# Quarter-array local products and a reordered preparation in the recurrence of an attention/RWKV-7 encoder

## The reference, cut to what matters

```python
decay = exp(-exp(-softplus(-(w0 + tanh(w_l) @ w2)) - 0.5))
a = sigmoid(a0 + a_l @ a2)
kk = heads(k * k_k);  kk = kk / max(sqrt(sum(kk * kk, -1)), 1e-12)
k = k * (1.0 + (a - 1.0) * k_a)
y = wkv7(r, decay, k, v, -kk, kk * a)
# wkv7, for each frame and head:
sa = einsum('hvk,hk->hv', state, at)
state = state * wt + sa (x) bt + vt (x) kt
y_t = einsum('hvk,hk->hv', state, rt)
y = group_norm(y) * ln_w + ln_b + sum(r * k * r_k, -1) * v
```

## Time and profile before

| | before |
|---|---|
| timed runs, median (lowest, highest) | 1804.3 us (1803.42, 1804.86) |
| the profiled execution's own time | 1807.21 us |
| its span, mean granted TensorE clock | 1805.4 us, 0.979 |
| TensorE busy | 1738.3 us, 96% |
| VectorE busy | 988.2 us, 55% |
| ScalarE busy | 796.3 us, 44% |
| GpSimd busy | 693.3 us, 38% |
| chain that ended last, by engine | PE 85%, DVE 7%, DMA 3%, ACT 3%, issue 2% |

### The profile page before, as it was taken

The page is one execution under the profiler, slowest core; times in us unless marked ns, Lnnn a source line. Parts: engine busy times, 40 slices in busy tenths (PEclk is TensorE's granted clock), DMA queues, the critical chain, the costliest instruction groups (busy, mean ns, idle before and its releaser), DMA issues.

```text
span 1805.4 us, 30026 instructions
## 1 busy us (share of the span) xinstructions
PE 1738.3 (96%) x11960; PEld 1321.0 (73%) x11960; DVE 988.2 (55%) x1551; ACT 796.3 (44%) x1519; POOL 693.3 (38%) x502
## 2 busy tenths in 40 slices
PE   7999999999998998999999999999999999999997
PEld 4766666665575766768888768878888888888886
DVE  6543232325464756453340462388856775884788
ACT  5313233235342443541120232467666666756763
POOL 2211202010120111223333103398686876968772
PEclk9999999998989999999999999999999999999999
DMA  5101000000212114051211102202202022030202
GB/s 206 47 24 33 22 35 13 21 5 18 54 20 43 26 40 110 27 205 38 79 47 49 33 0 65 75 25 70 77 29 83 24 70 66 28 93 25 70 1 93
DMA packets 81681, 94.36 MB, mean 52 GB/s; under 512 B 53648, under 2 KB 56208, under 8 KB 81552
## 3 DMA queue, kind: packets, MB, share of 16 engines
q1 hardware_dynamic: 81552, 92.56, 16.7%
HBM read 82.57 MB, written 9.98 MB: 51 GB/s over the span
## 4 chain that ended last, share of the span: by engine, by line
PE 85%; DVE 7%; DMA 3%; ACT 3%; issue 2%; POOL 1%; SPq 1%; DVEq 0%; ACTq 0%; POOLq 0%
PE PS L1652 33%; PE PS L934 16%; PE PS L994 8%; PE PS L1095 3%; PE PS L1113 2%; PE PS L1134 2%; PE PS L1599 2%; PE PS L1168 1%; PE PS L1577 1%; PE PS L1444 1%; PE PS L1459 1%; DMA xt_dram<-sc_s 1%; PE PS L1171 1%; PE PS L1359 1%; PE PS L1302 1%
## 5 line engine op out<-in xcount | busy, mean ns | idle before, releaser
L1652 PE MATMUL PS<-memr,wsp 128*128 128x512 f32 x1332 | 319.9, 391 | 2.4 <-POOL wsp L895 2.4
L934 PE MATMUL PS<-xn,wsp 128*128 128x512 f32 x1344 | 309.1, 391 | 6.7 <-DVE xn L2212 6.7
L934 PEld LDWEIGHTS PS<-xn,wsp 128*128 128x128 f32 x1344 | 252.8, 189 | 62.8 <-DVE xn L2212 5.9
L1652 PEld LDWEIGHTS PS<-memr,wsp 128*128 128x128 f32 x1332 | 249.7, 188 | 57.7 <-POOL wsp L895 3.3
L776 POOL CAST wsp<-wraw 128x1024 fp32r<-128x1024 f32 x40 | 42.7, 1068 | 468.8 <-PE PS L934 302.3
L1652 PE MATMUL PS<-memr,wraw_r 128*128 128x512 f32 x684 | 165.7, 391 | 0.7 <-POOL wraw_r L895 0.7
L994 PE MATMUL PS<-xn,wsp 128*128 128x512 f32 x576 | 149.5, 407 | 3.3 <-DVE proj L2261 3.1
L895 POOL TENSOR_TENSOR wsp<-sa,wsp 128x512 fp32r<-128x512 f32 x86 | 115.2, 1342 | 89.9 <-ACT wsp L2103 89.8
L1652 PEld LDWEIGHTS PS<-memr,wraw_r 128*128 128x128 f32 x684 | 128.2, 188 | 29.1 <-POOL wraw_r L895 1.1
L994 PEld LDWEIGHTS PS<-xn,wsp 128*128 128x128 f32 x576 | 106.4, 192 | 41.4 <-issue 20.7
L1776 ACT ACTIVATE H<-PS,mst 128x128 f32<-128x128 f32 (+3 forms) x64 | 47.5, 743 | 184.9 <-DVE mst L2342 179.7
(11 more groups left out here) (349 smaller groups left out, 3170.3 us busy)
## 6 DMA issues: line engine op xcount, KB each, us to landing
wraw<-in_weights_dram SPq DMA_DIRECT2D x40, 512.0 KB, 3.6
sa<-in_weights_dram SPq DMA_DIRECT2D x32, 512.0 KB, 4.2
H<-in_x_dram SPq DMA_DIRECT2D x16, 512.0 KB, 6.7
sbx<-in_weights_dram SPq DMA_DIRECT2D x32, 256.0 KB, 2.9
sa<-in_weights_dram SPq DMA_DIRECT2D x32, 256.0 KB, 2.8
H<-in_weights_dram SPq DMA_DIRECT2D x8, 512.0 KB, 6.5
out_dram<-sbx SPq DMA_DIRECT2D x16, 256.0 KB, 2.1
a_dram<-H SPq DMA_DIRECT2D x16, 128.0 KB, 2.5
```

The source lines that it names most:

```text
L934: last = nc.tensor.matmul(PS[:, 2 * k + half, :], wsp[:, k, kt, a, :], src[:, at, b, HALF * half:HALF * half + HALF], start=(i == 0 and (a ...
L1652: last = nc.tensor.matmul(PS[:, g % PS_BANKS, :], w[:, a, win(k)], x[:, b, :], start=(k == 0 and (a, b) == (0, 0)), stop=(k == ROWS - 1 an ...
```

## The change

It has five parts.

1. **Local products.** In `local` the selection product of the other chunk took all 128 rows of the array at once (`slice(0, P)`). Now each selection product has 64 rows; the second one of each head moves out of `local` into a new step `other_r` behind both windows' `local`, which waits for `local`'s products by TensorE's own count `lo`. `other_r(b)` stands between `carry(a)` and `carry(b)`. The number of matmuls is the same, 16 a window.
2. **Order and engines of the preparation.** Slots and engines before → after: kk DVE 3 → ACT 9; na DVE 4 → ACT 3; b DVE 16 → POOL 13; rt POOL 17 → 14; kksq 5 → 4 (straight from the projection); ks0, ks1 6, 7 → 5, 6; kf 10 → 7; W, Wi 10, 11 → 8; wt 12 → 10; afirst 17 → 13; t1p, L 3 → 4; am 4 → 5; nkk 14 → 12; k2 5 → 13; al0 to al3 18–21 → 17–20; rk 21 → 22; x0, x1 24 → 23; substitution ends in 30 in place of 33; bonus 31, 32 → 33, 34. `beside_heads` follows.
3. **Function tables of ScalarE.** One table with both Ln and Exp is named ahead of the Ln in the head, before attention and in slot 6 of the preparation. The program's `ACT_TABLE_LOAD` instructions fall from 29 to 14. The load for tanh in pairs 1 to 3 now stands behind ScalarE's wait for lw0.
4. **Start of the recurrence.** Slots 0 to 3 of `beside(0, ..)` stand ahead of the doubling, on TensorE and VectorE, in place of between its steps.
5. **SyncE** waits for `tok{p-1}_7` before it loads `o_places[p]`, from pair 1 on.

```diff
-SUBST = {26: (0, 1, 2, 3), 27: (4, 5, 6, 7), 29: (8,), 30: (9,), 31: (10, 11), 32: (12, 13), 33: (14,)}
-BONUS = 31
+SUBST = {26: (0, 1, 2, 3), 27: (4, 5, 6, 7), 28: (8, 9, 10, 11), 29: (12, 13), 30: (14,)}
+BONUS = 33
@@ beside_heads
-                return ((0,), (1,), (2,), (3, 4), (5, 6), (7, 8, 9), (10, 11), (12, 13, 14), (15, 16, 17))[i]
-            return ((), (18, 19), (20, 21, 22), (24,), (), (26, 27), (29, 30, 31), (32, 33), ())[i - 9]
+                return ((0,), (1,), (2,), (3, 4), (5, 6), (7, 8, 9), (10, 11), (12, 13), (14, 15, 16))[i]
+            return ((), (17, 18), (19, 20), (21, 22, 23), (), (26, 27), (28, 29, 30), (33, 34), ())[i - 9]
@@ TensorE, local
-                    for c, rows in ((h, chunk(h)), (1 - h, slice(0, P))):
-                        last = nc.tensor.matmul(to_r(c), con[rows, C_SEL + CH * h:C_SEL + CH * h + CH],
-                                                rAR[p % 2][rows, w, 1, chunk(c)], start=False, stop=True)
-                last.then_inc(L_PE.sem, L_PE.one(f"ry{p}_{w}"))
+                    for c in range(2):
+                        from_k(h, c)
+                    last = from_r(p, w, h, h)
+                last.then_inc(L_PE.sem, L_PE.one(f"lo{p}_{w}"))
+
+            def from_r(p, w, h, c):
+                rows = slice(HD * h, HD * h + HD)
+                return nc.tensor.matmul(PS[0:HD, 2 + 2 * (w % 2) + c, CH * h:CH * h + CH],
+                                        con[rows, C_SEL + CH * h:C_SEL + CH * h + CH],
+                                        rAR[p % 2][rows, w, 1, chunk(c)], start=False, stop=(h != c))
+
+            def other_r(p, w):
+                r_at(L_PE, f"lo{p}_{w}")
+                for h in range(2):
+                    last = from_r(p, w, h, 1 - h)
+                last.then_inc(L_PE.sem, L_PE.one(f"ry{p}_{w}"))
@@ TensorE, the recurrence
+            for s in range(4):
+                beside(0, s)
             for lv in range(LEVELS):
                 for w in range(2):
                     double_q(lv, 0, w)
-                beside(0, 2 * lv)
                 for w in range(2):
                     double_z(lv, 0, w)
-                beside(0, 2 * lv + 1)
...
-                    for k, stage in enumerate((solve, local, carry)):
-                        for w in ab:
-                            stage(p, w)
-                        beside(p, t + 4 + k)
+                    for w in ab:
+                        solve(p, w)
+                    beside(p, t + 4)
+                    for w in ab:
+                        local(p, w)
+                    other_r(p, ab[0])
+                    carry(p, ab[0])
+                    other_r(p, ab[1])
+                    beside(p, t + 5)
+                    carry(p, ab[1])
+                    beside(p, t + 6)
@@ ScalarE, prep
-                if s == 5:
-                    r_at(P_DVE, f"kk_{n}")
+                if s == 3:
+                    r_at(P_ACT, f"ta1_{n}")
+                    nc.scalar.activation(rA, rA, ACT.Copy, scale=-0.5, bias=-0.5).then_inc(sem_, one("na"))
+                if s == 4:
...
-                    nc.scalar.activation(rBh[i], rKK, ACT.Square).then_inc(sem_, one("kksq"))
+                    nc.scalar.activation(rBh[i], proj[:, T_K + n, :], ACT.Square, scale=vech[:, 8 + n:9 + n]).then_inc(
+                        sem_, one("kksq"))
+                if s == 6:
+                    nc.scalar.preload_act_table_set("natural_log_exp_and_others")
```

More of the change, by code:

```diff
@@ L477, in build @@
                                            "rk0", "rk1"]))
-        P_ACT = Steps(sem("prep_act"), each(["tw0", "tw1", "ta0", "ta1", "kksq", "kl0", "kl1", "W", "kf", "Wi", "wt0", "wt1", "afirst"]))
+        P_ACT = Steps(sem("prep_act"), each(["tw0", "tw1", "ta0", "ta1", "na", "kksq", "kl0", "kl1", "kf", "W", "Wi", "kk", "wt0", "wt1", "afirst"]))
         P_DVE = Steps(sem("prep_dve"), each(
[L480 to L483, removed]
+            ["t1p", "L", "am", "nkk", "k2", "at", "bt", "kt", "al0", "al1", "al2", "al3", "rk", "x0", "x1"]
+            + [y for place in SUBST for j in SUBST[place] for y in (f"xm{j}", f"xa{j}")] + ["xt", "bv0", "bv1"]))
+        P_POOL = Steps(sem("prep_pool"), each(["b", "rt", "kh", "bh"]))
         O_PE = Steps(sem("post_pe"), each(["vs0", "vs1", "lg0", "lg1"]))
@@ new lines, in to_r, with to_y, from_b, from_k @@
+                def to_r(h, c):
+                    return PS[0:HD, 2 + 2 * s + c, CH * h:CH * h + CH]
+                def to_y(h, c):
+                    return PS[HD:P, 2 + 2 * s + c, CH * h:CH * h + CH]
+                def from_b(h, c, to, cols):
+                    nc.tensor.matmul(to, rPG[s][chunk(c), h, cols], rSC[s][chunk(c), h, 0, :], start=(h == 0), stop=False)
+                def from_k(h, c):
+                    return nc.tensor.matmul(to_y(h, c), rVZ[s][chunk(c), h, HD:P], rSC[s][chunk(c), h, 2, :],
+                                            start=False, stop=(h == 1))
@@ L1713, in _ @@
             act.wait_ge(eps_made, 1)
-            nc.scalar.activation(small[:, 41:42], small[:, 40:41], ACT.Ln)
             for half in range(2):
@@ L1831, in prep @@
                     nc.scalar.activation(rB[i][:, halves(s - 6)], PS[:, 7, :], ACT.Ln).then_inc(sem_, one(f"kl{s - 6}"))
-                if s == 10:
+                if s == 7:
+                    r_at(P_ACT, f"kl1_{n}")
+                    nc.scalar.activation(rB[i], rB[i], ACT.Exp, scale=-0.5).then_inc(sem_, one("kf"))
+                if s == 8:
                     r_at(P_DVE, f"L_{n}")
@@ L1837, in prep @@
                     nc.scalar.activation(rW, rWi, ACT.Exp, scale=-half_e).then_inc(sem_, one("W"))
-                    r_at(P_ACT, f"kl1_{n}")
-                    nc.scalar.activation(rB[i], rB[i], ACT.Exp, scale=-0.5).then_inc(sem_, one("kf"))
-                if s == 11:
                     r_at(P_ACT, f"W_{n}")
                     nc.scalar.activation(rWi, rWi, ACT.Exp, scale=half_e).then_inc(sem_, one("Wi"))
-                if s == 12:
+                if s == 9:
+                    nc.scalar.activation(rKK, proj[:, T_K + n, :], ACT.Copy, scale=vech[:, 8 + n:9 + n]).then_inc(
+                        sem_, one("kk"))
+                if s == 10:
                     if n >= 2:
```

93 lines of the change are left out of this document (39 added, 54 removed).

## The result

The changed kernel takes 1814.06 us (median of 5 runs, 1811.47 to 1821.45), the kernel before in the same comparison 1803.42 (5 runs, 1794.47 to 1804.86): ratio 1.0085, 95% interval 1.006 to 1.011. It is slower, by 10.6 us between the medians and by some 15 us as the ratio has it; 1785.5 was forecast. The profiled execution took 1814.06 us, its span is 1812.3, the mean clock 0.968. That is 6.9 us more than the profiled execution of the kernel before, which at 1807.21 us was itself slower than all five timed runs: the two traces show a part of the loss.

A forecast was written before the change was run, and what follows sets the result against it. TensorE's own products were taken to set the recurrence's pace, busy 257 of 285 us. Gains and losses summed to −18.8 us from the 1804.3 us median, giving 1785.5 us, range 1775 to 1797.

The forecast's parts named there:

- Moves to GpSimd: Recurrence preparation: b on GpSimd starts 6.8 us before bt needs it, so 0; up to 1 us a pair if late.
- Head: Start of the kernel: one table load of 1.28 us between Ln and Exp goes and counts whole, −1.3 us.
- The tanh load: Pairs 1 and 2: table load behind the lw0 wait, 1.28 us each; with na on ScalarE, +4.7 us (0 to +7).
- The local products: Sixteen groups in the recurrence: quarter form −1.1 us each, −17.6; 4.95 returns as waits, net −12.6 us.
- Pair boundaries: Solved blocks load before TensorE asks: three waits go, −7.55, half clock behind them, −6.7; together −14.2 us, upper bound 0.
- End of attention: Head 7, block 7: rk1 waits for bv0, +4.0 us (0 to +5.3), and half clock behind it, +1.7 (0 to 3.4).
- The stall: TensorE at the end of head 7: idle about 3.1 us before rk1, until VectorE's bv0 has read bank 7.
- Start of the recurrence: End of attention to first solve: 20.6 us in place of 20.9, −0.3 us (−3 to +3).
- The slower rival: Recurrence: more, shorter waits lower the clock; slower from a mean clock of 0.88, 1810 us or more; chance 0.04.
- five new waits: TensorE in the recurrence: own-count wait, ks1, al0, tanh and na, named as what could lower the clock.

The follow-up runs named there:

- e2_bdve: The changed kernel with b back on VectorE and rt back in slot 17 on GpSimd: 1796.8 us, ratio 0.9978.
- e9_rtfirst: The changed kernel with rt issued ahead of b on GpSimd (slot 12), b still on GpSimd: 1802.6 us, ratio 1.0017.
- e3: The changed kernel with rk0 and bv0 of pair 0 moved to query block 6 of head 7, one substitution slot to block 5: 1815.1 us, ratio 1.0073.
- e4: The changed kernel with the first four slots of the recurrence back between the doubling's steps on TensorE and VectorE: 1810.8 us, ratio 1.0069.
- e8: The changed kernel with rt alone back in slot 17, b still on GpSimd: 1814.9 us, ratio 1.0077.
- e13: The changed kernel with tanh's table named ahead of ScalarE's wait for lw0, nothing else: 1805.65 us, ratio 1.0032.
- e10_tanh: e2_bdve with tanh's table named ahead of ScalarE's wait for lw0, na staying on ScalarE: 1785.2 us, ratio 0.9915.
- e14_tables: The kernel before with one table for Ln and Exp named in slot 6 of ScalarE's preparation, nothing else: 1810.4 us against 1799.3, ratio 1.0063.
- e6_all: e2_bdve with tanh's table named ahead of the wait, na back on VectorE, and the edits of e3 and e4: 1782.75 us, ratio 0.9883.
- e11_oldlocal: e6_all with the old local products: 1799.65 us against 1801.6 for the kernel before, ratio 0.9991.
- e1_local: The kernel before with the quarter-form local products, other_r and their order from the change, nothing else: 1792.5 us against 1799.9, ratio 0.9957.

## Why the prediction was wrong

- **Moves to GpSimd.** This step failed worst. "GpSimd works 53 of 285 us, and b (some 2 us) starts four slots, 6.8 us, before bt needs it: 0", with an upper bound of 1 us a pair. Idle time of GpSimd was read as room. Undoing it gives 17 us (e2_bdve), 11 of them by freeing rt alone (e9_rtfirst). I had looked at neither what runs on VectorE at that time, nor what b's new wait holds up behind it in GpSimd's stream; the 1.90 us of L2212 beside L778 stood in the trace of the kernel before. The half clock goes with it. In the five kernels with both operations beside VectorE's (the changed one, e3, e4, e8, e13) TensorE waits 1.6 to 3.8 us for al0, and in 15 of 15 cases a half-clock stretch begins or goes on within 16 us; in the eleven others, with waits up to 1.4 us, in 1 of 33. An estimate for the changed kernel: 6.8 us of waits, and 12 us lost in the 16 us at clocks of 0.89, 0.68 and 0.68 behind them, 19 us against the 17 of the runs. The Trainium skill has the rule, on the page SBUF — State Buffer, section SBUF: two separate sides: VectorE with two SBUF inputs and GpSimd share a port pair under an exclusive lock, and the later of them stands still for the whole instruction. By that rule, the trace agrees: the 1.07 and 1.08 us above.
- **Head.** "−1.3 us" was 0. The load went, and the first projection starts 9.52 us behind the start of the row sums in place of 9.54: VectorE's product came to stand beside GpSimd's L778 for all its length. It is the same step, what runs on the engine beside, in a second place.
- **The tanh load.** The wait was right, 1.42 us for 1.3. Its price was not: "1.28 us" a pair was charged, and e2_bdve against e10_tanh shows 11.6 us for three, e14_tables 11 in the kernel before. The lower clock behind it, in 9 of 14 cases, is what the traces show in addition. An estimate from them is 1.4 us of wait and on average 4.1 lost to the clock, 11 us for the two pairs; I added a half-clock stretch to the end of attention and to none of these. By the figure of the Trainium skill for a load (page ScalarE: Activation LUTs, section What ACT_TABLE_LOAD costs) the two loads would have been 5.3 us, an estimate. Against it, tanh starts 0.02 us after the load's end here as well, and in the head the load starts 0.02 us after Ln's end, so the rows leave no room for the drain that the page states.
- **The local products.** The mechanism held and the size was too small: 1.5 us a group, not 1.1. That TensorE's gain would come back as waits was right too, at 4.95 us too cheap: of 24 us 17 arrive in e6_all, against e11_oldlocal, and 7.5 in e1_local.
- **Pair boundaries.** The wait went and the clock behind it stayed full (the boundaries at 649 and 724 us have no 5 us below 0.97 behind them). But the −14.2 cannot be found as a gain of its own: e11_oldlocal, with the boundary mended and without the quarter form, is no faster than the kernel before. The forecast added this term and that of the local products as if each stood alone; alone they give about 2 and 7.5 us, together 17. Why the boundary pays nothing by itself stays open: e11_oldlocal holds the rest of the change too, and its trace shows a recurrence 12.2 us shorter but an attention stage 3.9 us longer than the trace before.
- **End of attention.** The stall was right to 0.02 us (3.08 for 3.1). Its end came 8.6 us late, not 5.7, and that understates it: attention began 4.0 us early in this trace and took 12.6 us longer. 1.6 us of that is a half-clock stretch at 209 us in head 2, where nothing was changed. At 444 us, behind the collision beside head 6, TensorE waits 3.02 us for Exp in place of 1.01; before block 6's products 2.24 in place of 1.39; and behind the stall the clock stood at 0.59 for 8 us, 3.3 us lost where I had put 1.7. It is not the collision alone: e10_tanh, without it, has an attention stage 8.9 us longer than the trace before.
- **Start of the recurrence.** "−0.3" was +2.6, at the edge of its bounds; e4_start wins it back in its trace. The 1.95 us of L1142 were not "at the lower clock": 490 to 493 us of the kernel before are at 1.00.
- **The slower rival.** I gave the clock 4%, with 0.88 as the point from which it decides. It named five new waits, and two of them, al0 and tanh, are those behind which the clock fell; but al0's was put at 0.35 us where it came to 3.05 in two pairs of three. The clock came to 0.91, and the waits did the rest. A collision of two engines was not among the rivals. The sentence that no stretch of the trace before shows half clock behind waits that short overlooked 494 to 500 us, at 0.51, with no wait above 0.92 us in the 8 us ahead of it.

Taken together: with the collision and the load mended (e10_tanh, 1785.2 us) the kernel lands on the forecast of 1785.5, with errors in the terms that cancel. That is luck: the head and the boundary gave nothing of their own, attention took 8.9 us more in that trace where 5.7 was forecast, and the quarter form gave more. How much of each loss is the wait and how much the clock behind it is estimated above and not separated by a run: none here holds the clock.

## What to carry to other kernels

Before an operation with two SBUF inputs is moved to an idle GpSimd, look at what VectorE does in those microseconds, and at what is queued behind the new wait; a slot in a hand-written order moves nothing if the engine doesn't wait there. In a stretch where TensorE's products hang on one another through another engine, price a new wait of 1.3 us at several times that, here 5 to 6 us, since half clock stood behind it in 9 of 14 cases. Of two gains in the same chain, test each alone and both together before you add them. And a profile is one execution: compare its time with the median before a difference of some us between two traces is given a cause.

## What the runs showed of the hardware

- VectorE and GpSimd, each with two inputs from SBUF, did not work side by side in any row looked at: a 1.2 us operation of VectorE took 2.9, 3.4 and 4.5 us, ending 1.07 us after GpSimd's. It works both ways: GpSimd's rt took 3.35 us in place of 2.37, and L865's pair of operations took 2.17 us beside k2 and at and 1.18 alone.
- A wait of 1.42 us in a chain of low-rank products stood ahead of 17 us at a mean clock of 0.60; waits of 2.28 us for the state sum, beside dense products, at 630 us and 705 us, had no half-clock stretch behind them, and neither had the wait of 1.42 us at 656 us in the same chain. The length of a wait alone does not tell whether the clock falls.
- Naming a table ahead moves the load to where it stands in the program; left alone, it stands behind the wait of its function, in the chain.
